# Beginning the next projection's first two weight tiles inside the output stage

## What is computed

```python
hc = mod_norm(xc, norm_g[i], sh_c, sc_c)          # rms_norm(x, g) * (1 + scale) + shift
hl = mod_norm(xl, norm_g[i], sh_l, sc_l)
...
xc = xc + gt_c * finish(o_c, g_c, w_out[i])       # finish: (o * silu(gate)) @ w_out
xl = xl + gt_l * finish(o_l, g_l, w_out[i])
```

## Time and profile before

| | us |
|---|---|
| median of 3 runs | 4417.83 |
| lowest and highest run | 4413.62, 4420.65 |
| the profiled execution, time | 4415.21 |
| the profiled execution, span | 4413.4 |
| PE busy in the span | 3983.1 (90%) |
| DVE, ACT, POOL busy | 2742.6, 2401.5, 1258.6 |
| mean granted TensorE clock | 0.953 |

### The profile page before, as it was taken

How to read it: one execution, slowest core, us unless ns; L and a number is a source line. 1 busy time by engine, 2 the same in 40 slices (tenths; PEclk the granted TensorE clock), 3 DMA queues, 4 the chain that set the end, 5 groups by cost and what they waited for, 6 DMA issues and landing times. The chain is left out here.

```text
span 4413.4 us, 58591 instructions
## 1 busy us (share of the span) xinstructions
PE 3983.1 (90%) x20892; PEld 1949.1 (44%) x20892; DVE 2742.6 (62%) x3647; ACT 2401.5 (54%) x3162; POOL 1258.6 (29%) x875
## 2 busy tenths in 40 slices
PE   5997799999989989999998988888989779999998
PEld 1453244444445544444444554444444324444444
DVE  4325577777555738888745518888532447777754
ACT  2325367776634327878832317778332437777761
POOL 1000044343321204544512103333210103444442
PEclk7998799999999989999999989999999879999999
DMA  4124522322201332222111432332111361221211
GB/s 194 48 78 137 148 66 60 75 65 67 73 20 56 114 93 63 63 63 57 34 60 55 122 101 68 82 79 51 57 47 64 109 181 36 54 51 42 50 45 55
DMA packets 375328, 329.39 MB, mean 75 GB/s; under 512 B 247520, under 2 KB 295200, under 8 KB 373968
## 3 DMA queue, kind: packets, MB, share of 16 engines
q1 hardware_dynamic: 375120, 326.60, 26.7%
HBM read 235.30 MB, written 91.23 MB: 74 GB/s over the span
## 5 line engine op out<-in xcount | busy, mean ns | idle before, releaser
L698 PE MATMUL bank<-H_hilo,w_hilo 128*128 128x512 f16 (+1 forms) x6336 | 1150.4, 344 | 2.9 <-ACT z_ring L903 2.1
L1471 DVE TENSOR_REDUCE max_parts<-bank 128x1 f32<-128x512 f32 (+2 forms) x1536 | 965.0, 653 | 282.5 <-PE bank L1426 258.1
L1666 ACT ACTIVATE p_f<-bank 128x1024 f32<-128x1024 f32 (+2 forms) x768 | 742.0, 966 | 537.9 <-PE bank L1618 494.2
L1618 PE MATMUL bank<-q_slots,k_slots 96*128 96x512 f16 (+7 forms) x3968 | 937.3, 365 | 0.7 <-ACT p_hi L1670 0.5
L1737 DVE TENSOR_TENSOR p_lo<-p_f,p_hi 128x1024 f16<-128x1024 f32 (+2 forms) x624 | 758.3, 1218 | 169.0 <-ACT p_hi L1670 165.8
L698 PEld LDWEIGHTS bank<-H_hilo,w_hilo 128*128 128x128 f16 x6336 | 620.9, 98 | 533.7 <-issue 12.5
L1670 ACT ACTIVATE p_hi<-bank 128x1024 f16<-128x1024 f32 (+2 forms) x768 | 737.6, 960 | 0.0
L1426 PE MATMUL bank<-k_slots,q_slots 96*128 96x512 f16 (+4 forms) x1536 | 541.9, 382 | 106.5 <-DVE max_parts L1471 58.0
L1589 PE MATMUL bank<-p_hi,v_hi_ones 128*128 128x512 f16 (+2 forms) x1568 | 565.0, 361 | 30.7 <-DVE p_lo L1737 18.2
L1591 PE MATMUL bank<-p_hi,v_lo_zeros 128*128 128x512 f16 (+2 forms) x1568 | 565.3, 361 | 0.0
L1593 PE MATMUL bank<-p_lo,v_hi_ones 128*128 128x512 f16 (+2 forms) x1568 | 564.0, 361 | 0.0
(11 more groups left out here) (167 smaller groups left out, 3486.3 us busy)
## 6 DMA issues: line engine op xcount, KB each, us to landing
ada_w<-in_w_ada SPq DMA_DIRECT2D x48, 768.0 KB, 5.4
gate<-z_ring SPq DMA_DIRECT2D x32, 640.0 KB, 2.9
gate_rows<-gate SPq DMA_DIRECT2D x64, 320.0 KB, 4.0
q_slots<-q_mla SPq DMA_DIRECT2D x64, 240.0 KB, 3.2
k_mla<-hilo_out SPq DMA_DIRECT2D x64, 224.0 KB
k_slots<-k_mla SPq DMA_DIRECT2D x64, 224.0 KB, 4.4
v_hi_ones<-v_scratch SPq DMA_DIRECT2D x64, 224.0 KB, 2.9
v_lo_zeros<-v_scratch SPq DMA_DIRECT2D x64, 224.0 KB, 3.5
```

The costliest lines, as they stand in the source:

```text
L698: ins = pe.matmul(dst, lhs(a, k), rhs(b, k), start=(k == 0 and n == 0), stop=(k == nk - 1 and n == 2))
L1471: dve.tensor_reduce(mx[:, par, t, c:c + 1], MB[(b * NE + k) % 2][:, 0:n], AX.X, ALU.max).then_inc(s_red.h, 1)
L1618: ins = pe.matmul(dst, lhs, rhs, start=(m == 0), stop=(m == len(ops) - 1), skip_group_check=swa)
L1666: act.activation(p32[:, p % 2, 0:cols], src, ACT.Exp, scale=scale).then_inc(s_p32.h, 1)
```

## The change

The eight banks belong to the program now and not to each stage, so that what PE has written in one stage is still there in the next. At each of the three boundaries the output stage loads and converts two tiles of the next projection, into both slots of `first_w_hilo`, and earlier (turn 2 on ACT, turn 3 on DVE of the last range). Behind its last own tile PE begins tiles 0 and 1 of the projection for the ranges 0 and 1, which are normed by then, in the banks 0, 1, 3 and 4 in which the projection expects them; the sum over squares of the last range stands between the third and the fourth eighth of tile 0's range 1. The projection (`begun=True`) skips these and computes only range 2 of the tiles 0 and 1; it no longer loads tile 1. The first layer (`start`) and the last output stage keep their order.

```diff
@@ -104,6 +104,7 @@
         self.w0 = sb("first_w_hilo", [P, 2, 2, KD, P], F16)
+        self.banks = [self.top.enter_context(nc.psum_tensor(f"bank{b}", [P, 2, BANK], F32)) for b in range(4)]
         dram = lambda name, shape, dt: nc.dram_tensor(name, shape, dt).ap()
@@ -123,8 +124,7 @@
         sb = lambda name, shape, dt: stack.enter_context(self.nc.sbuf_tensor(f"{name}_{n}", shape, dt))
-        banks = [stack.enter_context(self.nc.psum_tensor(f"bank{b}_{n}", [P, 2, BANK], F32)) for b in range(4)]
-        return stack, sb, banks
+        return stack, sb, self.banks
@@ -412,14 +412,14 @@
         xn = sb("xn", [P, 4, BANK], F32)
-        nx = self.next_tile(sb, nxt)
+        nx = self.next_tile(sb, *nxt)
         loads, splits, stores = ([], [], []) if final else self.cached_keys(sb, kind, CK, cache)
...
         s_xn, s_hh, s_hl = [S("xn_even"), S("xn_odd")], S("h_hi"), S("h_lo")
-        s_out = S("y_out")
+        s_out, s_nl = S("y_out"), S("next_lo")
         s_ld, s_h, s_l, s_st = S("cache_landed"), S("cache_hi"), S("cache_lo"), S("cache_stored")
@@ -563,7 +563,7 @@
                                 h_hi(act, c - 1, k)
-                        if c == NC - 1 and t == 6 and nx:
+                        if c == NC - 1 and t == 2:
                             act.wait_ge(s_z.h, s_z.base + c * KD + 1)
@@ -598,7 +598,7 @@
                                 dve.tensor_tensor(lo, src, hi, ALU.subtract).then_inc(s_l.h, 1)
-                        if c == NC - 1 and t == 7 and nx:
+                        if c == NC - 1 and t == 3:
                             self.next_lo(dve, nx)
@@ -648,7 +648,26 @@
                             sums(c - 1)
-                sums(NC - 1)
+                if final:
+                    sums(NC - 1)
...
+                def begin_next(t, c, k0, k1):
...
+                    pe.wait_ge(s_nl.h, s_nl.base + t + 1)
+                    pe.wait_ge(s_hl.h, s_hl.base + KD * (c + 1))
+                    pe.wait_ge(s_ev.h, s_ev.base + NC * KD - NZ + 3 * t + c + 1)
+                    t0, n = TOK_CHUNKS[c]
+                    for k in range(k0, k1):
+                        for m, (a, b) in enumerate(((0, 0), (0, 1), (1, 0))):
+                            pe.matmul(flat[3 * t + c][:, 0:n], self.w0[:, t, a, k], self.H[:, b, k, t0:t0 + n],
+                                      start=(k == 0 and m == 0), stop=(k == KD - 1 and m == 2))
+                if not final:
+                    begin_next(0, 0, 0, KD)
+                    begin_next(0, 1, 0, 3)
+                    sums(NC - 1)
+                    begin_next(0, 1, 3, KD)
+                    begin_next(1, 0, 0, KD)
+                    begin_next(1, 1, 0, KD)
         for b in range(SL):
@@ -664,31 +683,30 @@
-    def next_tile(self, sb, source):
-        return None if source is None else (sb("next_w_f32", [P, source.shape[1], P], F32)[:], source)
+    def next_tile(self, sb, *sources):
...
+        return [(sb(f"next_w_f32_{part}", [P, source.shape[1], P], F32)[:], source, self.w0[:, part, :, 0:source.shape[1]])
+                for part, source in enumerate(sources) if source is not None]
...
     def next_load(self, sp, nx):
-        if nx:
-            s_nx = self.sem("next_landed")
-            sp.dma_start(nx[0], nx[1]).then_inc(s_nx.h, 16)
+        s_nx = self.sem("next_landed")
+        for landing, source, _ in nx:
+            sp.dma_start(landing, source).then_inc(s_nx.h, 16)
...
     def next_hi(self, act, nx):
-        if nx:
-            s_nx, s_nh = self.sem("next_landed"), self.sem("next_hi")
-            act.wait_ge(s_nx.h, s_nx.base + 16)
-            act.activation(self.w0[:, 0, 0, 0:nx[0].shape[1]], nx[0], ACT.Copy, scale=W_SCALE).then_inc(s_nh.h, 1)
+        s_nx, s_nh = self.sem("next_landed"), self.sem("next_hi")
+        for landing, _, w in nx:
+            act.wait_ge(s_nx.h, s_nx.base + 16 * len(nx))
+            act.activation(w[:, 0], landing, ACT.Copy, scale=W_SCALE).then_inc(s_nh.h, 1)
...
     def next_lo(self, dve, nx):
-        if nx:
-            s_nh, s_nl = self.sem("next_hi"), self.sem("next_lo")
-            kt = nx[0].shape[1]
-            dve.wait_ge(s_nh.h, s_nh.base + 1)
-            dve.scalar_tensor_tensor(self.w0[:, 0, 1, 0:kt], nx[0], W_SCALE, self.w0[:, 0, 0, 0:kt],
-                                     ALU.mult, ALU.subtract).then_inc(s_nl.h, 1)
+        s_nh, s_nl = self.sem("next_hi"), self.sem("next_lo")
+        for n, (landing, _, w) in enumerate(nx):
+            dve.wait_ge(s_nh.h, s_nh.base + n + 1)
+            dve.scalar_tensor_tensor(w[:, 1], landing, W_SCALE, w[:, 0], ALU.mult, ALU.subtract).then_inc(s_nl.h, 1)
...
     def next_done(self, nx):
-        if nx:
-            self.sem("next_landed").done(16); self.sem("next_hi").done(1); self.sem("next_lo").done(1)
+        self.sem("next_landed").done(16 * len(nx)); self.sem("next_hi").done(len(nx)); self.sem("next_lo").done(len(nx))
@@ -724,7 +742,7 @@
         for t in range(-1, T):
-            for tile_ in range(1, depth) if t < 0 else [depth] if t == 0 else [t + depth - 1] if t > 1 else []:
+            for tile_ in range(2 if begun else 1, depth) if t < 0 else [depth] if t == 0 else [t + depth - 1] if t > 1 else []:
                 if tile_ < T:
@@ -1027,11 +1045,13 @@
                         pe.wait_ge(s_wlo.h, s_wlo.base + ready[t])
-                    w = wh[:, t % depth] if above_zero(t) else self.w0[:, 0]
+                    w = wh[:, t % depth] if t > (1 if begun else 0) else self.w0[:, t]
...
                     for c, (t0, n) in enumerate(chunks):
+                        if begun and t < 2 and c < 2:
+                            continue
                         ins = self.three(pe, Z[b][c], lambda s, k: w[:, s, k, :],
@@ -1877,7 +1897,7 @@
             else:
-                pr.out_norm(layer - 1, I["mla_in"][n][0], kind, CK, (I["c_ckv"][n], I["c_kpe"][n]))
+                pr.out_norm(layer - 1, [I["mla_in"][n][t] for t in range(2)], kind, CK, (I["c_ckv"][n], I["c_kpe"][n]))
             cq = ExitStack()
@@ -1893,7 +1913,7 @@
             pr.project(14, KD, I["mla_in"][n], lambda s, k, t0, m: pr.H[:, s, k, t0:t0 + m], TOK_CHUNKS, 5, groups, 1,
-                       I["mla_uq"][n][0])
+                       I["mla_uq"][n][0], begun=layer > 0)
             nope = [dict(tiles=[4 + j], stores=[
```

More of the change, by code:

```diff
@@ L396, in start, with out_norm @@
         stack.close()
-    def out_norm(self, layer, nxt=None, kind=None, CK=None, cache=None):
+    def out_norm(self, layer, nxt=(), kind=None, CK=None, cache=None):
         nc, I, S = self.nc, self.I, self.sem
@@ L700, in three, with project @@
         return ins
-    def project(self, T, KT, weights, rhs, chunks, ring_n, groups, slots, nxt, v_weights=None):
+    def project(self, T, KT, weights, rhs, chunks, ring_n, groups, slots, nxt, v_weights=None, begun=False):
         nc = self.nc
@@ L1202, in attention @@
         mrow = MLA_QK if mla else HD
-        nx = (self.sin[:, 0:KD * P].rearrange("p (k m) -> p k m", k=KD), nxt)
+        nx = [(self.sin[:, 0:KD * P].rearrange("p (k m) -> p k m", k=KD), nxt, self.w0[:, 0])]
         V = sb("v_hi_ones", [P, 2, NKT, P], F16)
@@ L1915, in build @@
             name = "gqa" if kind == 1 else "swa"
-            pr.out_norm(layer - 1, I[f"{name}_in"][0], kind, None, I[f"c_{name}_k"])
+            pr.out_norm(layer - 1, [I[f"{name}_in"][t] for t in range(2)], kind, None, I[f"c_{name}_k"])
             groups = []
@@ L1931, in build @@
             pr.project(18, KD, I[f"{name}_in"], lambda s, k, t0, m: pr.H[:, s, k, t0:t0 + m], TOK_CHUNKS, 5, groups, 2, None,
-                       I[f"{name}_v"])
+                       I[f"{name}_v"], begun=True)
             Q, K = head_slots()
```

## The result

| | us |
|---|---|
| before, median of 4 runs | 4419.24 (4413.62 to 4422.04) |
| with the change, median of 4 runs | 4365.81 (4364.20 to 4367.51) |
| ratio, with its 95% interval | 0.9884 (0.9871 to 0.9896) |
| span of the profiled execution, before and after | 4413.4, 4364.1 |
| mean granted TensorE clock, before and after | 0.953, 0.959 |

A forecast was written before the change was run, and what follows sets the result against it. TensorE, busy 90% of the span, was taken to bound the kernel, with little to gain except where it stands still. Savings of 16.9 + 16.9 + 16.4 = 50.2 us at three boundaries gave 4367.6 us, range 4360 to 4380.

The forecast's parts named there:

- Steps 1 and 2: Output stage's last range: earlier conversions delay VectorE's split 2.4 us, last add 1.2; TensorE's first piece costs the sum nothing.
- The stall that the bounds had spoken of: VectorE beside GpSimd: 0.95 us stall already there, at best swallowed by the new conversions, gain 53 in all.
- the worse bound: VectorE's two conversions each run into GpSimd's 1.27 us, the chain slips 2 to 3 more; 41 us gain in all.
- Rival A: Conversions and GpSimd hold each other up at the port, 3 us more per boundary; 4377 us, chance 0.12.
- Step 3: Norm's chain at the boundary: sum's start to VectorE's last split takes 11.7 us instead of 12.2, from a warm array.
- Step 4: TensorE's second piece, 63 matmuls, 13.6 us, ends last, 2.4 behind the norm; projection starts at 1318.2, 3.3 later than before.
- Step 5: Projection's start: rests take 5.3 us, tile 2 waits 2.2 for tile 0's banks, emptied behind two conversions; 17.0 saved per boundary.
- the clock should last through the wait: Projection's start: TensorE's clock stays up through the 2.2 us wait before tile 2; the 1.9 us cold start goes too.
- the weights would be late next: Projection's start: were ScalarE's bank copy put ahead of the conversions, tile 2's weights would be the next thing late.
- Rival B: ScalarE and VectorE set the projection's end, 17 us return as z_ring waits; 4418 us, no change, chance 0.03.
- Rival C: Clock falls to 1.2 GHz from the begun tiles to the rests of tiles 0 and 1; 4437 us, chance 0.03.
- Rival D: Begun matmuls run faster than 0.216 us, TensorE is through before the norm; gain 19.6 each, 4359 us, chance 0.04.

The follow-up runs named there:

- the conversions alone: The change without its begun matmuls: two tiles loaded and converted early, projection from scratch; 4418.90 us, ratio 0.9999 to the kernel before.
- the kernel with idle work: The kernel before plus 28 unread matmuls ahead of the last sum and 45 behind it at each boundary; 4410.56 us, ratio 0.9981.
- the combined one: The change with 12 matmuls left to the projection, tile 0 copied first, second conversion behind VectorE's last addition; 4360.02 us, again 4357.17.

## Why the prediction was right

**Steps 1 and 2** were right to 0.1 us. The split of range 1 ended 1301.33 + 0.68 - 1296.56 = 5.45 us after the own tiles (forecast 1301.5 - 1296.0 = 5.5), the sum started at 7.62 (7.6). That VectorE's whole backlog moves by what is put into it was shown by the conversions alone (7.6 as well). The stall that the bounds had spoken of came, but did not add up: at the first boundary the two conversions took 3.42 us instead of 2.42, GpSimd's multiplication beside them 2.11 instead of 1.27, and the addition behind them 0.60 instead of 1.38. The stall changed its place. The Trainium skill (SBUF — State Buffer, section "SBUF: two separate sides") has the exclusive lock, and the trace agrees with it: each engine was held up beside the other. It is the worse bound, a stall for each conversion on top of the old one, that the trace refutes. **Rival A** is out with it.

**Step 3:** the chain from the sum to the last split took 1316.16 - 1304.18 = 12.0 (11.7 forecast). The 0.3 come from GpSimd, whose last addition of the shift took 0.89 instead of 0.61, so that the others waited for longer; in the kernel with idle work both values occur, 11.7 and 12.0. What chooses between them isn't known. The norm lay off the path.

**Step 4:** the second piece ended last, as said, and the projection started 22.2 us after the own tiles, as forecast (1318.2 - 1296.0). That TensorE holds the barrier was shown by moving 12 of its matmuls across, which moved the barrier by 2.5 us.

**Step 5** was right in its mechanism (the copy of tile 0 behind two conversions: shown by the copy put first) and off in two terms. ScalarE could start on the first weights 4.5 us after the stage's start at the first boundary and not 3.7, so tile 2 came at 8.1 and not 7.5 after it; at the others it was 3.3 and 3.7, and 7.0 and 7.4. (In the kernel before it was 3.7, 3.9 and 3.3; the prediction had taken the first for all.) And "the clock should last through the wait" held in one profiled execution and not in the other, where it failed at two of three boundaries and cost 3 us. That the weights would be late next was right: with the copy ahead of the second conversion, tile 2 still waited 1.66, 0.29 and 0.80 us for what hangs on them.

**The size:** 50.2 forecast, 50.4 by the yardsticks of the profile. So close a match is partly luck: against the 29.7 forecast for each boundary the three were 0.6 over, 0.5 under and 0.1 under, and the execution profiled was one that kept its clock; the medians differ by 53.4. **Rival B** is out: from tile 2 on PE waits in the first projection after the boundary as before (3.0 us for `var_rstd`, 1.7 for z_ring, 2.1 before), and the waits for z_ring over the program are 34.9 against 35.7. **Rival C** is out for the begun work, at 1.00 in every window shown, though its mechanism appears in small behind waits. **Rival D** asked for matmuls faster than 0.216; 24 took 5.34 with their tail, and the Trainium skill's figure of 131 ns (TensorE: Matmul & The Clock Gate, section "Back-to-back issue gap") isn't met by any row here.

What stays open is the run-to-run spread in the stretches between the boundaries, which the yardsticks don't contain. The profiled executions show two pieces of it, each about 2 us: the clock behind short waits, and the wait of 1.6 or 3.8 us in an attention stage; why they fall one way or the other isn't shown.

## What to carry to other kernels

Where an engine stands still at the end of a stage because others finish the last piece, let it begin what the next stage does with the pieces already finished, and mind first where in its queue the operation stands that the others wait for: here that place alone was worth 35 of 53 us. Then look at the barrier again: begin so much that both sides arrive together (here 84 of the 96 matmuls; other amounts weren't tried), and let what is cut off cover the first wait behind it. A wait of 2 to 3 us on TensorE can cost 1.4 to 1.7 more through the clock.

## What the hardware showed that I had not expected

TensorE's granted clock fell after short waits in some executions and not in others: not after 2.73, 1.97 or the earlier trace rows 2.14 us, but after 2.89 and 2.22 (0.59 and 0.53 in the 3.6 us behind them), after 2.49 and 2.33 in the kernel with late conversions (0.51 and 0.55), after 2.77 in the one with the sum last (0.55) and after 1.99 in the combined one (0.61). The same wait for z_ring was 1.99 us with one tile begun too, and there the clock stayed at 1.00:

```profile
1516.35 39.10 PE L714 MATMUL bank<-H_hilo,w_hilo 128*128 128x512 f16 x216 [1.99 <-ACT z_ring L919]
```

So the length of the wait alone doesn't tell which; what does is not settled here. And an operation of VectorE that was held up beside GpSimd spared the one behind it its own stall (1.0 us more on the conversions, 0.8 less on the addition), so that the chain moved by the bare 2.4 us of work.
